# Samples' mixing stage: the order of its opening loads on two issuing queues

## The reference, cut to what matters

```
# matrix memory (4 heads): per sample a state C [v, k], a normaliser n and a running maximum m
q, k, v, o, gates = split(pa);  gates += mlstm_gate_b
num   = (q k^T * decay) v + w_inter * (C q)        # needs C, n and m of the sample
C, n  = dec * C + sum(wk * v k^T),  dec * n + sum(wk * k)
y_a   = sigmoid(o) * rmsnorm(num / den, mlstm_norm)

# RWKV-7 (4 heads): per sample a state S [v, k], and the last row for the token shift
pcs   = pc + rwkv_mu * (prev - pc)
decay = exp(-exp(w0 + tanh(pcs_w) @ w2 ...)); a = sigmoid(a0 + pcs_a @ a2); g = sigmoid(pcs_g) @ g2
kk    = normalise(k * k_k);  S = S * decay + (S a) b^T + v k^T   # over the 8 rows
y_c   = (groupnorm(S r) + bonus) * g
```

## Time and profile before

| what | us |
|---|---|
| median of 3 runs | 5799.68 |
| the three runs | 5804.31, 5795.87, 5799.68 |
| the profiled execution | 5798.44 |
| its span, first to last instruction | 5796.3 |

### The profile page before, as it was taken

One profiled execution on the slowest core, in us unless ns is written; L12 is line 12 of the kernel. 1 busy time (PEld: TensorE's weight loads), 2 busy tenths in 40 slices (PEclk: granted clock), 3 DMA queues, 4 the chain that ended last, 5 costly groups with the idle time before them and its releaser, 6 DMA issues. The chain is left out here.

```text
span 5796.3 us, 59972 instructions
## 1 busy us (share of the span) xinstructions
PE 4906.6 (85%) x22450; PEld 3134.3 (54%) x22474; DVE 2954.7 (51%) x6746; ACT 1518.7 (26%) x2877; POOL 298.4 (5%) x328
## 2 busy tenths in 40 slices
PE   5999777586688899989989996756766988999999
PEld 3344444455565488874443444435555655888643
DVE  2255454476874377760021545545778744777400
ACT  1232123257353100000012412233673521000000
POOL 1000232000000000001000002320000000000000
PEclk9999666576699999999989995565766999999999
DMA  8732432310002311227234324332100032111221
GB/s 287 248 102 79 122 101 84 79 31 17 11 24 89 123 55 65 67 91 276 79 102 130 113 77 115 104 98 54 31 17 21 17 115 102 67 60 67 83 69 52
DMA packets 372580, 510.47 MB, mean 88 GB/s; under 512 B 69779, under 2 KB 277205, under 8 KB 363637
## 3 DMA queue, kind: packets, MB, share of 16 engines
q1 hardware_dynamic: 325188, 367.15, 20.1%
q0 software_dynamic: 29696, 134.24, 7.2%
q10 hardware_dynamic: 17408, 5.25, 0.4%
HBM read 367.61 MB, written 149.08 MB: 89 GB/s over the span
## 5 line engine op out<-in xcount | busy, mean ns | idle before, releaser
L493 PE MATMUL pp<-w_in,nT 128*128 128x512 f32 x1792 | 803.2, 599 | 0.0
L493 PEld LDWEIGHTS pp<-w_in,nT 128*128 128x128 f32 x1792 | 330.0, 191 | 387.2 <-issue 387.1
L3509 PE MATMUL x<-nT,wgu 128*128 128x272 f32 x2112 | 510.7, 395 | 14.7 <-DMA wgu<-in_w_gate 14.7
L3739 PE MATMUL pm<-w_down,hT 128*128 128x512 f32 x1024 | 448.3, 596 | 28.5 <-DMA hT<-scratch_hT 28.5
L3509 PEld LDWEIGHTS x<-nT,wgu 128*128 128x128 f32 x2112 | 404.5, 192 | 99.7 <-DMA wgu<-in_w_gate 15.5
L3509 PE MATMUL x<-n_sum,w_sum 128*128 128x272 f32 x1408 | 341.4, 396 | 12.6 <-DVE n_sum L3568 12.6
L3739 PEld LDWEIGHTS pm<-w_down,hT 128*128 128x128 f32 x1024 | 195.3, 191 | 272.5 <-issue 272.5
L1904 POOL DMA_INDIRECT kv_sel<-in_cache_kv,kv_idx x256 | 247.3, 966 | 1412.5 <-DVE kv_idx L2048 1175.4
L3592 DVE RECIPROCAL exp_neg<-one_more 128x544 f32<-128x544 f32 x88 | 312.7, 3553 | 3.0
L3509 PEld LDWEIGHTS x<-n_sum,w_sum 128*128 128x128 f32 x1408 | 270.2, 192 | 69.7 <-issue 13.4
L3805 DVE TENSOR_TENSOR x_tile<-pm,x_tile 128x512 f32<-128x512 f32 x32 | 22.2, 693 | 538.2 <-PE pm L3739 538.2
(11 more groups left out here) (716 smaller groups left out, 8526.7 us busy)
## 6 DMA issues: line engine op xcount, KB each, us to landing
scratch_pages<-page_quarters POOLq DMA_DIRECT2D x32, 1024.0 KB, 8.6
area<-scratch_pages SPq DMA_DIRECT2D x64, 512.0 KB, 5.7
w_in<-in_w_in SPq DMA_DIRECT2D x14, 2048.0 KB, 8.6
scratch_hT<-hT SPq DMA_DIRECT2D x44, 544.0 KB, 2.9
wgu<-in_w_gate SPq DMA_DIRECT2D x22, 1024.0 KB, 5.4
wgu<-in_w_up SPq DMA_DIRECT2D x22, 1024.0 KB, 5.4
hT<-scratch_hT SPq DMA_DIRECT2D x16, 1408.0 KB, 8.1
w_down<-in_w_down SPq DMA_DIRECT2D x16, 1024.0 KB, 15.4
```

The costliest lines, as they stand in the source:

```text
L493: ins = pe.matmul(pp[u % 2][:, 0:cw], nT[:, k, t * P:(t + 1) * P], w[:, k, 0:cw], start=(k == 0), stop=(k == KT - 1))
L3509: ins = pe.matmul(out[:, j, :], left[:, k, :], right[:, k, j * QN:(j + 1) * QN], start=(k == 0), stop=(k == HK - 1))
L3739: ins = pe.matmul(pm[b][n][:, :], h[b][:, k, :], weights(k, slice(n * 512, (n + 1) * 512)), start=(k == 0), stop=(k == FT - 1))
```

## The change

In the samples' stage two queues get another order. SyncE issues RWKV's two row loads and its eleven constants first, and the matrix memory's five loads behind them, still ahead of the four tile loads. ScalarE issues RWKV's eight state loads first and the matrix memory's eight behind them. No instruction, wait or transfer is added or removed, and the order of the strands' steps on all engines stays.

```diff
@@ -3183,17 +3183,17 @@
         with nc.Block() as block:
             @block.sync
             def _(sp):
-                m_loads(sp)
                 r_loads(sp)
                 rows.load_rows(sp, l, io)
+                m_loads(sp)
                 for t in range(2):
                     rows.load_tile(sp, sc, t)
                 walk(order, r_sync(sp), m_sync(sp))
 
             @block.scalar
             def _(act):
+                r_states(act)
                 m_states(act)
-                r_states(act)
                 walk(order, r_scalar(act), m_scalar(act))
                 m_store(act)
 
```

## The result

The changed kernel takes 5815.36 us in the median of seven runs against 5799.68 of seven of the kernel before: a ratio of 1.0029, with a 95% interval of 1.0020 to 1.0038, so 11.6 to 22 us slower. The profiled execution has a span of 5810.6 us.

The account below looks back on a forecast made before the run. Full DMA engines bound the two layers' openings, which ScalarE's issues and the last constant end. m_rows_in's +3.7 and +4.5 (+8.2) plus 0.4 us a layer gave +9.0, so 5808.7 us; range 5798 to 5816.

Parts of the forecast that it names:

- RWKV's earlier rows: SyncE's queue: rows start 2.76 us sooner, worth nothing because their reader lora_in stands behind m0.
- the two delays: Each layer's opening: m_rows_in's and m_C's late landings don't add; the later one counts.
- m_C as a floor of its own: Tail of ScalarE's queue: +2.2 us in each layer even if m_rows_in were free, up to 2 us more possible.
- The 0.4 us a layer: Added to m_rows_in's delay because its range and that of m_C's delay overlap.
- the size of m_rows_in's delay: qkT in layers 0 and 1: +3.7 and +4.5 us, sum +8.2, ends +5.4 to +11.0.
- the 2.76: SyncE's queue runs up to 2.76 us ahead, since the small loads no longer stand first; the middle was taken.
- rival (c): Openings: m_rows_in or m_C lands with the very last load; +7.8 and +7.8 us, 5815.3 us; chance 0.21.
- (a): SyncE doesn't stall before its fourteenth issue, m_rows_in lands 3.8 us after issue; +0, 5799.7 us; chance 0.13.
- (b): Openings shorten by the 2.76 us of small issues in each layer; -5.5 us, 5794.2 us; chance 0.04.
- The clock: 25 us behind each opening: TensorE's busy time may fall otherwise to the 2.4 GHz piece, up to 1.75 us a layer.
- the 0.6 us: Opening: VectorE's spare time before ScalarE asks for its reduction; kk at most 0.8 us later, covered by ScalarE's 3.7 us delay.
- up to 2 us more: m_C's tail on ScalarE's queue: possible extra delay over +2.2 us, as 256-byte pieces share engines with larger packets from the start.

Follow-up runs that it names:

- the order by need: Kernel before with loads ordered by need, then SyncE's m_rows_in, RWKV's rows, mu, small loads, rest: stages 113.0 / 112.3 us; 5783.97 against 5789.85 us, ratio 0.9990.

## Why the prediction was wrong

It said "within 0.2%" as the likeliest (5808.7 us), and gave slower by more 0.30. The kernel is slower by 0.29% (0.20 to 0.38), with the median just inside the range of 5798 to 5816.

**What held.** Where the change acts, and that RWKV's earlier rows are worth nothing: VectorE's shift began 7.5 us after the stage's start instead of 11.0, and the wait moved into its m0. The sign, the place (qkT's wait turned from issue to TensorE's transposes of m_rows_in), that all behind shifts as a whole, and that the two delays don't add. m_C as a floor of its own: forecast +2.2 to +4.2 a layer, measured +3.2 / +3.8 when it was alone. With SyncE's order it is hidden: it landed at 24.5 and was wanted at 27.3. The 0.4 us a layer that I added for it were wrong in kind.

**The step that failed** is the size of m_rows_in's delay, +3.7 and +4.5 with ends of +5.1 and +5.9; it was +7.8 and +10.6. I had read its landing off a position in bytes, 18.9 / 18.2 us after the start, and then took 1.4 us off, half of the 2.76 by which SyncE's queue was to run ahead: 17.5 / 16.8. It landed at 21.5 / 22.8. First, the head start didn't come: m_rows_in was issued at 12.5 / 12.7, where rwkv_a was issued at 12.1 / 12.1, since SyncE's stalls come sooner as well, and in its first 16 us SyncE's queue moved 2.44 / 2.33 MB against 2.28 / 2.37 before. Secondly, and this is the larger part, 2.6 / 4.6 us: the 18.9 / 18.2 were the landing of the queue's last load but one, and m_rows_in is at its end, where ScalarE's pieces weigh most. With all of these held it lands at 16.3 / 17.1. That this is close to my 17.5 / 16.8 is chance, since my reading had ScalarE's traffic in it. Bytes ahead were a fair measure further forward in the queue (with 1024 and 1536 KB ahead m_rows_in landed within 1 us or so of what was expected) and the wrong one at its end. The row for the end stood there: rwkv_a took 9.3 us and landed 2.7 us behind rwkv_w, 1.9 in layer 1. I used it for rival (c) alone.

**Rival (c)** gave +7.8 and +7.8, with 0.21. Layer 0 is this case: m_rows_in landed at 21.5, where the last constant had landed before. Layer 1 is 2.8 us beyond it, with a landing at 22.8 where that constant's was at 20.0. That (c)'s total, 5815.3, is the measured median is luck: it has 15.6 us for the two stages, which lost 19.8. (a) was right in one thing: the fourteenth issue comes at 8.0 us if nothing stalls, as with all states held; but the load then still takes 8.2 / 8.9 us and not 3.8. (b) didn't occur.

**The clock** term, up to 1.75 us a layer either way, was 1.1 in layer 0 and nothing in layer 1.

**VectorE**: m_n landed at 24.4 / 25.1, not 21.6 / 20.1, but it stayed covered by ScalarE's delay, as said. With m_rows_in alone moved to the front that cover was gone, and lora_in's transposes were 4.2 / 5.5 us late by the small loads. VectorE also had more to spare than the 0.6 us that I read: ScalarE loads its table for the root before it asks for VectorE's result, and asked at 1048.10 and not at 1046.79, so 1.9 us. (With the steps in another order the root began 0.04 us after VectorE's reduction, the table long loaded.)

**Smaller things.** Eleven issues, not twelve, lie before SyncE's wait for the zeroed wa2. The "up to 2 us more" for m_C's tail had no row behind it; the tail came some 1 us later than s_S's had.

The rule of the Trainium skill that I named ("DMA: Bandwidth & Descriptors", "Issuing engines are not separate DMA queues") bore out further than I took it: the last loads of SyncE's queue are late by ScalarE's traffic, and in some orders the last of ScalarE's by SyncE's tiles. What I drew from it, no gain in total from sorting a queue, doesn't follow and is wrong for the stage: the order by need made it 3.9 / 3.0 us shorter.

## What to carry to other kernels

In an opening that is bound by DMA, a load's place must follow the order in which the engines' queues meet their waits, over all strands, and not the strand that one wants to speed up. Before a load is moved back, look at what stands behind the wait for it on its engine, and price it by the landing of the queue's last loads and not by its middle. Loads of the next stage that follow on the same queue aren't free either: they can hold back the end of another engine's queue.

## What the runs showed of the hardware

- SyncE's and ScalarE's loads share the DMA engines, and small pieces can lose: with SyncE's tile loads (rows of 4 KB) issued ahead of it, ScalarE's last 64 KB load, in pieces of 256 bytes, took 12.9 / 12.6 us to land, and 5.2 / 5.2 us with those held. In the kernel before, where ScalarE's last load was issued first, the hold changed its landing by less than 1 us.
- SyncE's queue, with ScalarE's held, brought 2434 KB in 16.3 / 17.1 us. A load at its end took 8.2 / 8.9 us from issue to landing then, and 9.0 / 10.1 in the changed kernel; most of what the held queue gave is that the load was issued at 8.0 us and not at 12.5. At the front a load of 258 KB took 3.6 to 4.0.
- Issuing isn't free for an engine that also computes: ScalarE's sixteen issues held it for 14.8 / 13.3 us in the kernel before, with single ones of 2.7 us. With eight of them moved behind two short steps the first of these steps ran 9.3 / 7.9 us sooner.
